# Norms of a three-block sequence kernel: sums of squares as one column per 128 tokens, means in four strips

## The reference

```python
def layer_norm(x, g, b):
    mu = jnp.mean(x, axis=-1, keepdims=True)
    var = jnp.mean(jnp.square(x - mu), axis=-1, keepdims=True)
    return (x - mu) * lax.rsqrt(var + 1e-5) * g + b

def rmsnorm(x, g):
    return x * lax.rsqrt(jnp.mean(x * x, axis=-1, keepdims=True) + 1e-6) * g

h = layer_norm(x, ln_in_g, ln_in_b)
for l in range(2):
    # token_mix holds a layer_norm over the 256 channels of its convolution
    h = layer_norm(ALPHA * h + token_mix(h, ...), ln1_g[l], ln1_b[l])
    h = layer_norm(ALPHA * h + conv_ffn(h, ...), ln2_g[l], ln2_b[l])
```

## Time and profile before

| what | us |
|---|---|
| median of three executions | 3735.51 |
| their range | 3733.14 to 3737.32 |
| the profiled execution's own time | 3739.27 |
| its span, from the first to the last instruction | 3737.5 |
| mean granted TensorE clock, as a share of 2.4 GHz | 0.922 |

### The profile page before, as it was taken

One profiled execution on the slowest core, in us unless ns is written; L12 is line 12 of the kernel. 1 busy time (PEld: TensorE's weight loads), 2 busy tenths in 40 slices (PEclk: granted clock), 3 DMA queues, 4 the chain that ended last, 5 costly groups with the idle time before them and its releaser, 6 DMA issues. The chain is left out here.

```text
span 3737.5 us, 66286 instructions
## 1 busy us (share of the span) xinstructions
PE 3191.7 (85%) x28285; PEld 2513.8 (67%) x28285; DVE 1989.7 (53%) x2750; ACT 1124.0 (30%) x1783; POOL 1043.7 (28%) x608
## 2 busy tenths in 40 slices
PE   4998899999699988999855996799999978399886
PEld 2875567878476556887624884688888866279634
DVE  3678747860477874883204740566666632431252
ACT  2224424331323343332213221333333212322221
POOL 0322134544122222554200220444344311022100
PEclk7999899999899999999967998899999998799988
DMA  2331122333222122333171332000000021021101
GB/s 69 79 79 46 45 69 85 97 93 88 65 64 78 40 63 67 92 98 90 54 274 52 112 98 109 16 4 20 20 20 20 8 77 45 17 79 57 51 0 68
DMA packets 354104, 243.93 MB, mean 65 GB/s; under 512 B 22212, under 2 KB 330872, under 8 KB 353164
## 3 DMA queue, kind: packets, MB, share of 16 engines
q1 hardware_dynamic: 350398, 231.57, 20.7%
q10 hardware_dynamic: 3406, 8.04, 0.6%
HBM read 222.54 MB, written 17.04 MB: 64 GB/s over the span
## 5 line engine op out<-in xcount | busy, mean ns | idle before, releaser
L571 POOL TENSOR_TENSOR weights_lo<-weights_raw,weights_hi 128x1024 fp32r<-128x1024 f32 (+1 forms) x234 | 595.7, 2546 | 1151.4 <-ACT weights_hi L540 1151.4
L1167 PE MATMUL psum<-moving_hi,weights_hi 128*128 128x512 f32 x1488 | 609.0, 409 | 108.4 <-DVE weights_lo L571 61.3
L1167 PE MATMUL psum<-moving_lo,weights_hi 128*128 128x512 f32 x1488 | 589.0, 396 | 0.0
L1167 PE MATMUL psum<-moving_hi,weights_lo 128*128 128x512 f32 x1488 | 588.3, 395 | 0.0
L1167 PEld LDWEIGHTS psum<-moving_hi,weights_hi 128*128 128x128 f32 x1488 | 285.2, 192 | 226.2 <-issue 71.2
L540 ACT ACTIVATE weights_hi<-weights_raw 128x1024 fp32r<-128x1024 f32 (+2 forms) x250 | 253.7, 1019 | 280.5 <-PE psum L1167 240.4
L1167 PEld LDWEIGHTS psum<-moving_hi,weights_lo 128*128 128x128 f32 x1488 | 285.0, 192 | 61.8
L1167 PEld LDWEIGHTS psum<-moving_lo,weights_hi 128*128 128x128 f32 x1488 | 285.9, 192 | 59.2 <-issue 4.9
L2436 POOL TENSOR_TENSOR second_off<-second_mats,second_masks 128x256 f32<-128x256 f32 x180 | 141.1, 786 | 183.8 <-PE psum L1881 183.8
L1167 PE MATMUL psum<-hn_hi,even_hi 128*128 128x256 f32 (+1 forms) x480 | 162.9, 339 | 34.1 <-DVE even_lo L571 34.1
L571 POOL TENSOR_TENSOR even_lo<-even_raw,even_hi 128x1024 fp32r<-128x1024 f32 x28 | 67.4, 2408 | 362.8 <-ACT even_hi L540 362.8
(11 more groups left out here) (430 smaller groups left out, 6890.1 us busy)
## 6 DMA issues: line engine op xcount, KB each, us to landing
weights_raw<-in_w_up SPq DMA_DIRECT2D x88, 512.0 KB, 3.9
weights_raw<-in_w_in SPq DMA_DIRECT2D x78, 512.0 KB, 3.8
ada_raw<-in_ada_w SPq DMA_DIRECT2D x12, 2048.0 KB, 18.6
odd_raw<-in_od_w_in SPq DMA_DIRECT2D x16, 1024.0 KB, 5.5
even_raw<-in_ev_w_in SPq DMA_DIRECT2D x30, 512.0 KB, 3.9
weights_raw<-in_w_down SPq DMA_DIRECT2D x32, 448.0 KB, 3.7
weights_raw<-in_w_o SPq DMA_DIRECT2D x16, 512.0 KB, 4.3
weights_raw<-in_w_down SPq DMA_DIRECT2D x16, 512.0 KB, 4.2
```

Source lines behind the costliest of these rows:

```text
L571: ops.tensor_tensor(self.ring.lo[i % n][:, a:b], self.ring.raw[:, t % self.ring.landing, a:b], self.ring.hi[i % n][:, a:b].bitcast(F32), A ...
L1167: return nc.tensor.matmul(to, (hi, lo)[which][:, at:at + P], moving(k)[part], start=start and k == 0 and i == 0, stop=stop and k == n_k - ...
```

## The change

It changes how all 11 norms get the reciprocal of the root, and how five of them get the mean.

- **Sums by token.** The squares become the stationary operand, in blocks of 128 tokens, and one column of the mean table is the moving one. The result is a column with the tokens on the partitions, one column for each 128 tokens, each in a bank of its own (`sum_by_token`). Eps, root and reciprocal are done on these 4 or 6 columns (`Deviation`).
- **Spreading.** For each block TensorE multiplies the column, repeated 128 times as the stationary operand, with the identity, which gives the reciprocal of each token in all rows, in PSUM (`to_all_rows`). The multiplications read it there. `norm_stats` copies it to `stats` with ScalarE.
- **Means in strips** (`layer_norm`, `norm_stats`). Each chunk is multiplied with 32 columns of the mean table, into the strip k % 4 of the partitions; ScalarE copies the four strips to SBUF; a product with a new 128x128 table `strips`, which picks one row of each strip, adds them up in all rows.
- **Order.** `warm` runs a root of one column at the head of ScalarE's list in each such stage. In `between` two of the four subtractions of `o` go ahead of the multiplications and two behind.
- The input table of constants has 128 columns more.

```diff
+    t["strips"] = np.tile((p[:, None] % 32 == 0).astype(float), (1, P))
...
+def sum_in_strips(nc, out, mean_w, x, K):
+    for c in range(K):
+        ps = slice(32 * (c % 4), 32 * (c % 4) + 32)
+        last = nc.tensor.matmul(out[ps, :], mean_w[:, 0:32], x[:, c, :], start=c < 4, stop=c >= K - 4)
+    return last
+
+def sum_by_token(nc, out, mean_w, x, start, stop):
+    for b in range(x.shape[1] // P):
+        last = nc.tensor.matmul(out[:, b:b + 1], x[:, b * P:(b + 1) * P], mean_w[:, 0:1], start=start, stop=stop)
+    return last
+
+def to_all_rows(nc, out, column, ident):
+    for b in range(column.shape[1]):
+        last = nc.tensor.matmul(out[:, b * P:(b + 1) * P], column[:, b:b + 1].to_broadcast([P, P]), ident, start=True, stop=True)
+    return last
+
+class Deviation:
+    def __init__(self, nc, sems, psum, bank, rstd_bank, ident, column, n, eps):
...
+        end = 512 * rstd_bank + (n * P + 511) // 512 * 512
+        self.sums = psum.rearrange("p (b n) -> p b n", n=512)[:, bank:bank + n, 0]
+        self.rstd = psum[:, end - n * P:end]
+        self.column, self.spare = column[:, 0:n], column[:, 7:8]
+    def warm(self):
+        self.nc.scalar.activation(self.spare, self.ident[:, 0:1], ACT.Sqrt)
+    def dve(self, dve):
+        dve.wait_ge(self.summed, 1)
+        self.nc.vector.tensor_scalar(self.column, self.sums, self.eps, None, ALU.add).then_inc(self.safe, 1)
+        dve.wait_ge(self.root, 1)
+        self.nc.vector.reciprocal(self.column, self.column).then_inc(self.inverted, 1)
+    def act(self, act):
+        act.wait_ge(self.safe, 1)
+        self.nc.scalar.activation(self.column, self.column, ACT.Sqrt).then_inc(self.root, 1)
+    def pe(self, pe):
+        pe.wait_ge(self.inverted, 1)
+        to_all_rows(self.nc, self.rstd, self.column, self.ident).then_inc(self.spread, 1)
...
 def layer_norm / norm_stats, TensorE
-            for c in range(K):
-                last = nc.tensor.matmul(mean, mean_w, x[:, c, :], start=c == 0, stop=c == K - 1)
-            last.then_inc(mean_ready, 1)
+            sum_in_strips(nc, strips, common["mean_d"], x, K).then_inc(strips_ready, 1)
+            pe.wait_ge(strips_taken, 1)
+            nc.tensor.matmul(mean, common["strips"], scratch, start=True, stop=True).then_inc(mean_ready, 1)
             for c in range(K):
                 pe.wait_ge(squared, c + 1)
-                last = nc.tensor.matmul(var, mean_w, sq[:, c, :], start=c == 0, stop=c == K - 1)
-            last.then_inc(var_ready, 1)
+                last = sum_by_token(nc, dev.sums, common["mean_d"], sq[:, c, :], c == 0, c == K - 1)
+            last.then_inc(dev.summed, 1)
+            dev.pe(pe)
...
 norm_stats, ScalarE
+            dev.warm()
+            act.wait_ge(strips_ready, 1)
+            nc.scalar.activation(stats, strips, ACT.Identity).then_inc(strips_taken, 1)
             for i in range(ahead.split):
                 ahead.hi(act, i).then_inc(hi_made, 1)
             for c in range(K):
                 act.wait_ge(centered, c + 1)
                 nc.scalar.activation(sq[:, c, :], x[:, c, :], ACT.Square).then_inc(squared, 1)
-            act.wait_ge(var_safe, 1)
-            nc.scalar.activation(stats, stats, ACT.Sqrt).then_inc(std_ready, 1)
+            dev.act(act)
+            act.wait_ge(dev.spread, 1)
+            nc.scalar.activation(stats, dev.rstd, ACT.Identity)
...
 between, VectorE
-            dve.wait_ge(var_ready, 1)
-            V.tensor_scalar(stats, var, 1e-5, None, ALU.add).then_inc(var_safe, 1)
-            for c in range(4):
+            dev.dve(dve)
+            for c in range(2):
                 dve.wait_ge(o_rounded, c + 1)
                 rest(4 + c, o[:, c, :])
-            dve.wait_ge(std_ready, 1)
-            V.reciprocal(stats, stats).then_inc(rstd_ready, 1)
-            dve.wait_ge(rstd_ready, 1)
+            dve.wait_ge(dev.spread, 1)
             for c in range(2):
-                V.tensor_tensor(conv[:, c, :], conv[:, c, :], stats, ALU.mult).then_inc(scaled, 1)
+                V.tensor_tensor(conv[:, c, :], conv[:, c, :], dev.rstd, ALU.mult).then_inc(scaled, 1)
+            for c in range(2, 4):
+                dve.wait_ge(o_rounded, c + 1)
+                rest(4 + c, o[:, c, :])
...
 rms_norm
+            dev.warm()
...
-                    last = nc.tensor.matmul(psum[:, a:b], mean_d, sq[:, c, a - lo:b - lo], start=c == 0, stop=c == KD - 1)
-            last.then_inc(sum_ready, 1)
+                    last = sum_by_token(nc, dev.sums[:, a // P:b // P], common["mean_d"], sq[:, c, a:b], c == 0, c == KD - 1)
+            last.then_inc(dev.summed, 1)
+            dev.pe(pe)
...
-            nc.vector.tensor_scalar(stats[:, 0:hi - lo], psum[:, lo:hi], EPS2, None, ALU.add).then_inc(safe, 1)
-            dve.wait_ge(root, 1)
-            nc.vector.reciprocal(stats[:, 0:hi - lo], stats[:, 0:hi - lo]).then_inc(rstd_ready, 1)
-            dve.wait_ge(rstd_ready, 1)
+            dev.dve(dve)
+            dve.wait_ge(dev.spread, 1)
```

More of the change, by code:

```diff
@@ L281, in _ @@
                     .then_inc(transposed, 1)
-def layer_norm(nc, x, sq, stats, psum, mean_w, gain, bias, eps, silu=False, parts=None):
+def sum_in_strips(nc, out, mean_w, x, K):
[7 more added lines that the diff above has]
+    return last
@@ L288, in layer_norm @@
+def layer_norm(nc, x, sq, scratch, column, psum, common, gain, bias, eps, parts):
     K, T = x.shape[1], x.shape[2]
-    mean, var = psum[:, 0:T], psum[:, 512:512 + T]
-    with stage(nc, "mean_ready centered squared var_ready var_safe std_ready rstd_ready scaled result_ready rounded") as (block, sems):
-        mean_ready, centered, squared, var_ready, var_safe, std_ready, rstd_ready, scaled, result_ready, rounded = sems
+    strips, mean = psum[:, 0:T], psum[:, 512:512 + T]
+    with stage(nc, "strips_ready strips_taken mean_ready centered squared scaled result_ready rounded " + Deviation.NAMES) as (block, sems):
+        strips_ready, strips_taken, mean_ready, centered, squared, scaled, result_ready, rounded = sems[:8]
+        dev = Deviation(nc, sems[8:], psum, 2, 6, common["ident"], column, T // P, eps)
@@ L343, in norm_stats @@
+def norm_stats(nc, x, sq, stats, column, psum, common, eps, ahead):
     K, T = x.shape[1], x.shape[2]
-    mean, var = psum[:, 0:T], psum[:, 512:512 + T]
-    with stage(nc, "mean_ready centered squared var_ready var_safe std_ready hi_made") as (block, sems):
-        mean_ready, centered, squared, var_ready, var_safe, std_ready, hi_made = sems
+    strips, mean = psum[:, 0:T], psum[:, 512:512 + T]
+    with stage(nc, "strips_ready strips_taken mean_ready centered squared hi_made " + Deviation.NAMES) as (block, sems):
+        strips_ready, strips_taken, mean_ready, centered, squared, hi_made = sems[:6]
+        dev = Deviation(nc, sems[6:], psum, 2, 6, common["ident"], column, T // P, eps)
@@ L348, in _ @@
         @block.tensor
         def _(pe):
-            for c in range(K):
-                last = nc.tensor.matmul(mean, mean_w, x[:, c, :], start=c == 0, stop=c == K - 1)
-            last.then_inc(mean_ready, 1)
+            sum_in_strips(nc, strips, common["mean_d"], x, K).then_inc(strips_ready, 1)
+            pe.wait_ge(strips_taken, 1)
+            nc.tensor.matmul(mean, common["strips"], stats, start=True, stop=True).then_inc(mean_ready, 1)
             for c in range(K):
                 pe.wait_ge(squared, c + 1)
-                last = nc.tensor.matmul(var, mean_w, sq[:, c, :], start=c == 0, stop=c == K - 1)
@@ L767, in _ @@
                 pe.wait_ge(squared, c + 1)
-                last = nc.tensor.matmul(var, mean_w, sq[:, c, :], start=c == 0, stop=c == 1)
-            last.then_inc(var_ready, 1)
+                last = sum_by_token(nc, dev.sums, mean_w, sq[:, c, :], c == 0, c == 1)
+            last.then_inc(dev.summed, 1)
+            dev.pe(pe)
         @block.scalar
         def _(act):
+            dev.warm()
             for c in range(2):
@@ L1546, in first_block_layer @@
             ahead = Ahead(nc, ring, loads, split=1)
-            between(nc, pool_in, pool_w, layer(w["pool_w"], l), pool_y, conv, o, queries[:, 0:2, :], stats[:, :], psum,
-                    common["mean_conv"], col, parts, ahead)
+            between(nc, pool_in, pool_w, layer(w["pool_w"], l), pool_y, conv, o, queries[:, 0:2, :], column[:, :], psum,
+                    common, col, parts, ahead)
             next_tiles = Ahead(nc, ring, ffn_loads, split=2)
@@ L1642, in modulation, with rms_norm @@
                   also_pe, also_dve, also_act, "turned taken", raw_tiles=range(tiles))
-def rms_norm(nc, pieces, sq, stats, psum, mean_d):
-    with stage(nc, "squared sum_ready safe root scaled rstd_ready") as (block, sems):
-        squared, sum_ready, safe, root, scaled, rstd_ready = sems
-        n = len(pieces)
-        spans, done = [], 1024 - sum(x[0].shape[2] for x in pieces)
+def rms_norm(nc, pieces, sq, column, psum, common):
+    with stage(nc, "squared scaled " + Deviation.NAMES) as (block, sems):
```

(2 more changed lines are left out.)

112 lines of the change are left out of this document (55 added, 57 removed).

## The result

The changed kernel takes 3753.7 us (median of five executions, 3752.6 to 3754.2) against 3735.2 us for the kernel before (3732.1 to 3737.3, five executions beside it): 1.005 times the time, 95% interval 1.0036 to 1.0065, 18.4 us slower. Forecast was 3751.5, or +16.

A forecast was written before the change was run, and what follows sets the result against it. It read each norm as a chain of engine steps, TensorE being busiest. Two `layer_norm` -1.4, two `norm_stats` +0.2, first norm +1.3, `between` -5.4, `rms_norm` +21.0, table +0.3 gave +16.0: 3751.5 us, 8 in 10 from 3739 to 3762.

The forecast's parts named there:

- The level: In the sums by token, one moving column doesn't hold the high clock: 0.116 us a record high, 0.22 low.
- Rival 1: In the sums by token, the high clock holds, 64 records cost 7.4 us: -46.5 us, 3689 us; chance 0.09.
- The point of the fall: In the sums by token, the clock falls 3.9 us after the last wide product; rows show 2.0 to 5.2.
- The low record: In sums by token at the low clock level, one record takes 0.22 us, bounds 0.21 to 0.23.
- The strips: In the means of five norms, 3.77 us replaces 7.14, -3.4 each; first norm 6.4 us, -3.6.
- The tail: From last sum to multiplication, 2.7 us replaces 4.8 for 512 columns, 3.6 replaces 6.9 for 768: -2.1 and -3.3.
- The stages: Per norm: `layer_norm` -0.7 us, `norm_stats` +0.1, first norm +1.3, four `rms_norm` +6.4, +5.6, +5.8, +3.2.
- `between`: In both layers, the column chain ends earlier and VectorE's queue sets the end: -2.7 us each, bounds -2.4 and -3.1.
- the larger constant table: In the input constants, 64 KB more, claimed to cost +0.3 us.

## Why the prediction was right, and where its terms were off

**The level.** The argument that decided the sign holds: narrow records by token don't keep the clock up, even with TensorE busy for 13.0 of 13.0 us. The Trainium skill, "TensorE: Matmul & The Clock Gate", "Why this matters for your kernels", asks for TensorE without gaps; the windows of the changed kernel and of the one with 32 columns show a gapless stream at 0.50, and the one with 128 columns shows a stream with the same weight loads rising to 1.00. Rival 1 had a price of 3689 for a high level in the sums. With 128 columns, which bring it about, the kernel took 3692, so the pricing of the level was sound to some 3 us, though in five of its nine long sums the clock was at 0.50 for the first 3 or 4 us, where the rival had that in two; what was wrong with rival 1 is only that one column doesn't bring it.

**The point of the fall** is the term that was mis-sized. I took 3.9 us after the last wide product in all norms, though the rows that I had showed it between 2.0 and 5.2. In the changed kernel it was 1.7, 1.9, 1.8 and 2.3 us in the four norms of the layers, 3.0 and 2.2 in `rms_norm` 2 and 4. So the layers' sums took 13.6, 13.4, 13.5 and 13.1 us for my 11.9, and the last `rms_norm` 13.4 for 12.2. The strips are most of the difference in the layers: behind them it was 1.6 to 2.4 us in all twelve norms of the three profiled kernels with 1 or 32 moving columns (the changed one, the one with `rms_norm` taken back, the one with 32 columns), and behind a full mean 5.1 to 5.4 us in six norms of eight, but 2.4 and 2.0 in the other two. In `rms_norm` 2 and 4, with no strips ahead, it was 3.8 and 2.8 in the kernel with full means and 4.0 and 2.8 in the one with 32 columns. What sets it beside the strips stays open.

**The low record** took 0.215 us (20.64 / 96), in place of 0.22. This gave back 0.5 us in each `rms_norm` over 768 columns that starts low: 20.6 for 21.1.

**The strips** were right where nothing else hangs on them: the subtraction 3.79 us after the start for 3.77, and 6.46 in the first norm for 6.4. What they cost in the level behind them was at nothing in the sum: by the run with full means, up to 3.1 us in a norm's narrow sums.

**The tail** was right: 2.8 us from the last sum to the multiplication for 2.7, and 3.7 for 3.6 over 768 columns.

**The stages.** `layer_norm` +0.9 and +0.6 us for -0.7; `norm_stats` +1.8 and +1.6 for +0.1; the first norm +1.1 for +1.3; the `rms_norm` +5.9, +5.8, +5.3 and +4.4 for +6.4, +5.6, +5.8 and +3.2. The misses above half a microsecond are the point of the fall. That of the first norm is small by chance: the same code gave sums of 11.15 us in another profile.

**`between`** gained 3.4 and 3.3 us, for 2.7 with bounds of 2.4 and 3.1, so outside of them. To compare with my times, add 1.40 us to those of the changed kernel, in which the stage starts that much earlier, as its first work on VectorE shows (before, L797, then changed, L855):

```profile
430.45 1.28 DVE L797 TENSOR_TENSOR conv<-conv,psum 128x512 f32<-128x512 f32 x2 [2.31 <-PE psum L758]
...
429.05 1.28 DVE L855 TENSOR_TENSOR conv<-conv,psum 128x512 f32<-128x512 f32 x2 [2.31 <-PE psum L815]
```

Three terms were each a little long. The multiplication starts at 437.84 for my 438.0 to 438.6; ScalarE's table load ends at 439.6 for my 440.1; and VectorE, without a gap from the multiplication on, ends at 443.9 for my 444.9, or 444.2 at the far bound. Alone the part is worth 6.5 us for two. The timeline of the changed kernel in `between`, layer 0:

```profile
436.44 1.28 DVE L865 TENSOR_TENSOR conv<-conv,psum 128x512 f32<-128x512 f32 x2 [0.15 <-PE psum L303]
436.91 1.28 ACT L846 ACT_TABLE_LOAD   x1
438.20 1.52 ACT L846 ACTIVATE conv<-conv,columns 128x512 f32<-128x512 f32 x2
...
441.19 1.28 DVE L798 TENSOR_TENSOR moving_lo<-conv,moving_hi 128x512 fp32r<-128x512 f32 x2
442.77 0.77 PE L1225 MATMUL psum<-moving_hi,weights_hi 128*128 128x512 f32 x1 [6.37 <-PEq L188]
```

**The sum.** The eleven stages add up to +20.7 us in the profiled executions, for my +16.0: 6.1 us more in the four norms of the layers, most of it the earlier fall, and 0.4 in the `rms_norm`, less 1.3 for `between`, 0.2 for the first norm, and the 0.3 of the larger constant table, which no row shows (the first norm starts 0.2 us earlier, not later). The spans show +13.6. The other 7 came back in stretches whose code is the same, none of them more than 2.3 us (59 to 428 us -2.3, the second block's even layer from 1995 to 3186 us -2.0, the modulation -1.3), one of them the other way (960 to 1329 us, +1.5). 4 us of it may be no more than that the profiled execution of before lay above its median. The rest has no cause that a run shows. That the median came out 2.2 us from the forecast is thus partly luck: falls that came early, against time that came back where nothing was changed.

## What to carry to other kernels

Where a product turns to few moving columns, price its records at both clock levels and look up in the trace which level such a stream keeps, since a busy engine is no sign of a high clock. If the weight load sets a record's time, give the moving operand more columns, for here 128 cost nothing per record and brought the clock up, worth 62 us, where 32 brought nothing. Summing in four strips before turning to token columns did away with most of the records, worth another 17. When a phase is made shorter, read the clock just behind it: the strips gained 3.4 us where they stand and cost 1.6 us in the next products with 128 columns and 3.1 with one (both `norm_stats`, layer 0). A term that a single profile shows can move by 3 us with the point at which the clock falls, so price it at both ends of what the rows show.

## What the runs showed of the hardware that was not expected

- 1 and 32 moving columns behind the same weight load gave the same time, 3753.7 us both, and 0.50 in all long sums after 4 us at most; 128 raised a clock that had already fallen, within the sums, in the first norm, in `norm_stats` and in the third `rms_norm`.
- With narrow records behind a mean in the layers the fall came between 1.6 and 5.4 us after the last wide product, and varied between stages of one execution: sums of 10.4 and 13.3 us with the same records and the same full mean ahead.
- Wide products put between the narrow ones, about half of the time, left the clock at 0.50 for 16 us in one stage and at 1.00 for 18 and 13 us in two others. That kernel had a spread of 44 us between executions, the one with 256 columns 5.
- Profiled executions can lie at an end of their kernel's range (3721.6 in one of 3722 to 3731, 3746.2 in one of 3746 to 3760), so a part of under 10 us is better taken from medians, and its place from the trace.
